# State-space groups: output products of the third and fourth pair, norm and scaling in a later slot, scaling placed behind the products of the inputs

## The reference

```python
proj = h @ in_w                                  # z, xBC, dt
xBC = silu(causal_depthwise_conv(xBC, conv_w, conv_b))   # 4 taps
xs, Bm, Cm = split(xBC)
dt = softplus(dt + dt_bias);  A = -exp(A_log)
# one chunk of 256 tokens per sequence, for each group and head:
cb = einsum("blgn,bsgn->blsg", Cm, Bm)
y = einsum("blsgk,bsgkp->blgkp", cb[..., None] * decay, xs * dt[..., None])
y = (y + xs * D_skip) * silu(z)
yg = y.reshape(bsz, L, 8, -1)                    # 512 features per group
yg = yg * rsqrt(mean(square(yg), -1) + eps);  y = yg * norm_g
return y @ out_w
```

## Time and profile before

| | |
|---|---|
| time, median of 3 runs | 3548.23 us (3548.18 to 3550.38) |
| time of the profiled execution | 3549.42 us |
| its span | 3547.6 us |
| PE / PEld busy | 3447.0 us (97%) / 3381.8 us (95%) |
| DVE / ACT / POOL busy | 2783.1 us (78%) / 1987.5 us (56%) / 587.2 us (17%) |
| mean granted clock of TensorE | 0.995 of full speed |
| part of the span with the state-space groups 1 to 7 and the projections behind them | about 2275 to 2895 us |

### The profile page before, as it was taken

The page is one execution under the profiler, slowest core; times in us unless marked ns, Lnnn a source line. Parts: engine busy times, 40 slices in busy tenths (PEclk is TensorE's granted clock), DMA queues, the critical chain, the costliest instruction groups (busy, mean ns, idle before and its releaser), DMA issues.

```text
span 3547.6 us, 68240 instructions
## 1 busy us (share of the span) xinstructions
PE 3447.0 (97%) x27858; PEld 3381.8 (95%) x27858; DVE 2783.1 (78%) x4529; ACT 1987.5 (56%) x3204; POOL 587.2 (17%) x546
## 2 busy tenths in 40 slices
PE   7999999999999999999999999999999998999997
PEld 7999999999999998999999999999999998999997
DVE  7788888577797887877888887898989867666665
ACT  6555546566547676565555546665656746434344
POOL 2111112111113011131111112231313300000000
PEclk9999999999999999999999999999999999999999
DMA  6555556444465444655555565556464543555552
GB/s 239 217 197 219 217 227 231 176 155 179 165 251 203 172 169 173 267 185 218 201 221 202 208 262 180 178 175 230 171 233 169 186 169 146 210 189 199 204 190 107
DMA packets 113688, 699.61 MB, mean 197 GB/s; under 512 B 13216, under 2 KB 29792, under 8 KB 31456
## 3 DMA queue, kind: packets, MB, share of 16 engines
q1 hardware_dynamic: 104128, 685.14, 52.2%
q10 hardware_dynamic: 8784, 8.46, 1.0%
q0 software_dynamic: 464, 1.64, 0.1%
HBM read 684.64 MB, written 2.16 MB: 194 GB/s over the span
## 4 chain that ended last, share of the span: by engine, by line
PE 49%; DVE 13%; ACT 6%; issue 2%; DMA 1%; POOL 1%; DVEq 0%; SPq 0%; POOLq 0%; ACTq 0%
PE g L446 15%; PE g L448 15%; PE g L447 15%; DVE w_lo L1594 4%; ACT w_hi L1026 2%; DMA w_raw<-in_slots 1%; POOL scratch L2409 1%; DVE vec L2095 1%; DVE rstd L2095 1%; PE turn_bank L485 1%; DVE scratch L1659 1%; DVE scratch L2121 0%; DVE scratch L2129 0%; PE norm_bank L459 0%; DVE h L2225 0%
## 5 line engine op out<-in xcount | busy, mean ns | idle before, releaser
L1594 DVE TENSOR_TENSOR w_lo<-w_raw,w_hi 128x1024 fp32r<-128x1024 f32 x1088 | 1337.0, 1232 | 433.9 <-ACT w_hi L1026 423.1
L1026 ACT ACTIVATE w_hi<-w_raw 128x1024 fp32r<-128x1024 f32 x1088 | 1129.6, 1053 | 873.2 <-PE g L448 761.7
L446 PE MATMUL g<-p_hi,w_hi 128*128 128x256 f32 x4576 | 1318.0, 288 | 36.4 <-DVE w_lo L1594 23.2
L448 PE MATMUL g<-p_hi,w_lo 128*128 128x256 f32 x4576 | 1296.2, 283 | 0.0
L447 PE MATMUL g<-p_lo,w_hi 128*128 128x256 f32 x4576 | 1296.2, 283 | 0.0
L446 PE MATMUL g<-q_hi,w_hi 128*128 128x256 f32 x3408 | 980.0, 288 | 5.7 <-DVE w_lo L1594 2.2
L448 PE MATMUL g<-q_hi,w_lo 128*128 128x256 f32 x3408 | 964.0, 283 | 0.0
L447 PE MATMUL g<-q_lo,w_hi 128*128 128x256 f32 x3408 | 963.8, 283 | 0.0
L446 PEld LDWEIGHTS g<-p_hi,w_hi 128*128 128x128 f32 x4576 | 879.1, 192 | 46.1 <-DVE w_lo L1594 32.7
L447 PEld LDWEIGHTS g<-p_lo,w_hi 128*128 128x128 f32 x4576 | 879.3, 192 | 1.4
L448 PEld LDWEIGHTS g<-p_hi,w_lo 128*128 128x128 f32 x4576 | 879.0, 192 | 0.0
(11 more groups left out here) (445 smaller groups left out, 3929.2 us busy)
## 6 DMA issues: line engine op xcount, KB each, us to landing
w_raw<-in_slots SPq DMA_DIRECT2D x640, 1024.0 KB, 4.9
scratch<-scratch SPq DMA_DIRECT2D x128, 64.0 KB, 4.9
scratch<-s_rows ACTq DMA_DIRECT2D x16, 256.0 KB, 3.4
con<-s_rows ACTq DMA_DIRECT2D x16, 256.0 KB, 5.1
h<-in_x SPq DMA_DIRECT2D x4, 512.0 KB, 6.2
out_h<-h SPq DMA_DIRECT2D x4, 512.0 KB, 2.6
sq<-in_p POOLq DMA_DIRECT2D x4, 256.0 KB, 3.0
con<-in_consts SPq DMA_DIRECT2D x1, 832.0 KB, 10.7
```

The source lines that it names most:

```text
L446: pe.matmul(g, wh, hi[:, k], start=n == 0, stop=False)
L448: last = pe.matmul(g, wl, hi[:, k], start=False, stop=n == len(ks) - 1)
L1026: act.activation(w_hi[k % SPLIT][:, cols], raw[MAIN_AT[k] % RAW][:, cols], ACT.Copy).then_inc(hi_ready, 1)
L1594: dve.tensor_tensor(w_lo[k % SPLIT][:, cols], raw[MAIN_AT[k] % RAW][:, cols], w_hi[k % SPLIT][:, cols], SUB).then_inc(lo_ready, 1)
```

## The change

The steps of the group before are moved, for groups 1 to 7. `S_OUT`, the steps in which the four output products (and the sums, squares and additions behind them) are done, goes from (0, 1, 3, 4) to (0, 1, 4, 5). The norm (PE, and ACT's `factor`) goes from step 5 to 6, `s_scale_y` (DVE) and `s_y_hi` (ACT) from step 6 to 7, `s_y_lo` (DVE) from the start of step 7 to the start of step 8. In step 7 DVE does `s_previous`, that is, the scaling, behind `s_inputs` and no longer ahead of it. For the last group's work, which is done during the last projection, the steps stay as they were (`S_OUT_TAIL`). No instruction is added or removed; each engine has as many rows as before. In the changed program the lines of the functions are 2 to 8 higher.

```diff
--- before.py
+++ after.py
@@ -137,7 +137,7 @@
 
 LN_TILES = [[] if n < 6 else [2 * n - 12, 2 * n - 11] if n < 12 else [n] for n in range(DT)]
 
-S_OUT = (0, 1, 3, 4)
+S_OUT, S_OUT_TAIL = (0, 1, 4, 5), (0, 1, 3, 4)
 
 A_SLOTS = 8 * A_HEADS
 PLE_SLOTS = 1 + DT + 8 + 1 + 8
@@ -815,9 +815,11 @@
 
         def s_previous(g, step, turned):
 
-            if step in S_OUT:
-                s_out(S_OUT.index(step), turned)
-            if step == 5:
+            tail = g == S_GROUPS - 1
+            outs = S_OUT_TAIL if tail else S_OUT
+            if step in outs:
+                s_out(outs.index(step), turned)
+            if step == (5 if tail else 6):
                 s_norm()
 
         def s_norm():
@@ -1390,13 +1392,15 @@
                 last.then_inc(scaled_h, 1)
 
         def s_previous(g, step):
+            tail = g == S_GROUPS - 1
+            outs = S_OUT_TAIL if tail else S_OUT
             if step < 2:
                 s_fetch(g, step + 2)
-            if step in S_OUT:
-                s_square(S_OUT.index(step))
-            if step == 5:
+            if step in outs:
+                s_square(outs.index(step))
+            if step == (5 if tail else 6):
                 factor(rsn[:, 2], "eps_5")
-            if step == 6:
+            if step == (6 if tail else 7):
                 s_y_hi(g)
 
         def s_group(g):
@@ -2136,9 +2140,11 @@
             dve.tensor_tensor(q_lo[:, four], s_y, q_hi[:, four], SUB).then_inc(x_lo, 1)
 
         def s_previous(g, step):
-            if step in S_OUT:
-                s_y_out(g, S_OUT.index(step))
-            if step == 6:
+            tail = g == S_GROUPS - 1
+            outs = S_OUT_TAIL if tail else S_OUT
+            if step in outs:
+                s_y_out(g, outs.index(step))
+            if step == (6 if tail else 7):
                 s_scale_y(g)
 
         def s_steps(n):
@@ -2157,7 +2163,7 @@
 
         def s_group(g):
             for n in range(10):
-                if g and n == 7:
+                if g and n == 8:
                     s_y_lo(g - 1)
                 begin()
                 if g == 0:
@@ -2165,10 +2171,12 @@
                 x = take(columns=n == 1 and g in (3, 5))
                 dve.tensor_copy(s_xbp[:, n % 2, 3:3 + SEQ] if n < 6 else s_z[:, n - 6], x).then_inc(tile_taken, 1)
                 lo_half(1)
-                if g:
+                if g and n != 7:
                     s_previous(g - 1, n)
                 if 4 <= n <= 7:
                     s_inputs(g, n - 4)
+                if g and n == 7:
+                    s_previous(g - 1, n)
                 if n < 6:
                     s_conv(g, n)
                 else:
@@ -2523,11 +2531,11 @@
             else:
                 pool.tensor_tensor(acc[:], acc[:], rsn[:, m % 2], ADD).then_inc(s_sum, 1)
 
-        def s_previous(step):
+        def s_previous(step, outs=S_OUT):
             if step in (2, 3):
                 s_weights(step)
-            if step in S_OUT:
-                s_add_square(S_OUT.index(step))
+            if step in outs:
+                s_add_square(outs.index(step))
 
         def s_group(g):
             for n in range(10):
@@ -2546,7 +2554,7 @@
             for g in range(S_GROUPS):
                 s_group(g)
             for step in range(5):
-                s_previous(step)
+                s_previous(step, S_OUT_TAIL)
 
             c.next("tile", 1 + 10 * S_GROUPS + DT * S_PAIRS)
             c.next("norm")
```

## The result

The changed kernel takes 3556.31 us (median of 11 runs, 3554.02 to 3559.43), the kernel before 3548.18 us beside it (11 runs, 3545.65 to 3550.38). The ratio is 1.0023, 95% interval 1.0015 to 1.0031: slower by 8.1 us. The profiled execution of the changed kernel took 3559.43 us, its slowest.

The account below looks back on a forecast made before the run. Two loops were taken as tight at once: PE's, and DVE and ACT's through the decay-row loads. Seven delays of 1.6 us less 2.9 us of slack gave +8.3 us, 3556.5 us; range 3549 to 3563.

Parts of the forecast that it names:

- Steps 1 and 2: PE's stalls before L812 (3.0 us) and at step 7's transposes (10.9 us) go; PE could gain 13.9 us.
- Step 3: Norm stays one step behind the fourth output product; costed at nothing in a first group.
- the circle: DVE and ACT loop from scaling through `q_hi`, decay-row loads, decay and `w_hi` to the next group: 65.47 us a group.
- Step 4: DVE's scaling comes 5.62 us later, behind the inputs of pairs 2 and 3 and other work.
- Step 5: On ACT the loads queue behind `s_y_hi`, which waits for the scaling: issued 1.84 us later, passed in full to the decay.
- d: Delay per group on DVE's and ACT's loop: 0.9 to 2.3 us, taken as 1.6.
- the slack of 0.93 us: DVE's waits for PE through ACT at step 1, taken off the delays: 0.40, 0.18, 0.35 us in groups 2, 4, 6.
- The sum: Delays over three segments of the layer, less slack: 2.8, 3.0 and 2.5 us, together +8.3 us.
- the 2.0 us of slack in the last projection: DVE's take of the second tile there could be 2.0 us late before PE's tile wanting it waits.
- Full gain, 3534.3: Rival: PE's stalls go and nothing takes their place, gaining all 13.9 us; chance 0.14.
- The lock gives time back, 3553: Rival: fewer DVE collisions with POOL at the new places, 0.9 to 1.2 us a group, +3.4 to +5.5; chance 0.14.
- New waits inside the group: Rival: PE late with step 7's tile delays the scaling by up to another 0.6 us a group, 3562; chance 0.10.

Follow-up runs that it names:

- e5: Changed kernel with decay-row loads issued in step 6 (groups 1 to 7), `s_y_hi` moved to step 8, `s_y_lo` to the start of step 9: 3534.65 us.
- e7: e5 with `q_lo` behind the take and low half of step 9, except in groups 2 and 4: 3537.71 us.
- e1: Changed kernel with ScalarE's two loads of decay rows in step 7 issued ahead of `s_y_hi`, not behind it: 3547.25 us.
- e8: Changed kernel run once more, unaltered: 3558.41 us.
- e4: Kernel before with only DVE's inputs of pair 2 put ahead of the scaling in step 6, nothing a step later: 3555.68 us.
- e6: Changed kernel with the scaling ahead of the inputs again, in its new step 7: 3555.33 us.
- e3: Kernel before with the first two loads of decay rows issued in step 6, ahead of `s_y_hi`, in groups 1 to 7: 3548.56 us.

## Why the prediction was right, point by point

The forecast was 3556.5 us; 3556.31 was measured, and the sum of +8.3 us against +8.1 by the medians and +8.7 by the stretch. That is closer than its terms deserve: two of them were off in opposite directions and nearly cancelled, which is luck.

- **Steps 1 and 2, what PE could gain.** 13.9 us. Right, and shown: e5 keeps the change, takes the loads and the copy out of the way, and its stretch is 13.9 us shorter.
- **Step 3, the norm at nothing in a first group.** Nearly: PE waits 3.9 us in five groups for the squares (L2532). While the circle is the longer loop these waits should cost nothing, since the circle's delay below is the whole loss; no run takes them out alone. In e7, where the circle is open, 2.8 us of such waits are nearly all that is left, and it is 3 us above e5.
- **Step 4, the scaling 5.62 us later.** The order of DVE's work was read rightly; the collisions took some off. From the output product to the end of the scaling it was 36.76 us in group 6 and is 2757.45 + 1.66 - 2717.43 = 41.68: 4.92 later. Of the 0.70 us that are missing, the scalings give 0.50 (2.16 to 1.66) and the inputs of pair 1 0.49, the inputs of pair 2 take 0.48 back, and DVE's wait for `w_hi` in step 2 is 0.17 shorter (0.74 for 0.91). The durations traded places as a lock has it.
- **Step 5, the loads behind the wait: d.** The mechanism is shown by e1. The size was 1.6 us a group, and it is smaller. The first decays of step 8 give it (the first table behind this list). From group 0 to group 7 they are 551.67 us apart before and 560.38 after: +8.71 us. With the slack of 0.93 us that was used up first, this is 9.64 / 7 = 1.38 us a group; in e8 it is 1.32. By the lock rule of the Trainium skill (SBUF — State Buffer, "Who interferes with whom") it was 1.35, nearer than my middle value. The seven steps are uneven: 1.87, 0.58, 1.90, 0.89, 1.45, 0.46 and 1.56 us. Those into groups 2, 4 and 6 have the slack in them; why the rest differ is open. Group 6 to group 7, from output product to output product, takes 66.3 us, not 67.1.
- **The sum.** Seven delays of 1.38 us less 0.93 give 8.7 us, and the stretch is 8.7 us longer: the circle's delay came through whole. The step that failed is the 2.0 us of slack in the last projection. DVE's take of the second tile there (L2186) was to be late by up to 2.0 us at no cost. The second table behind this list holds it against the end of the stretch. Where the clock does not fall at that place (e1, e4, e6), the stretch is longer by 1.5 to 1.6 us less than the take is late; in the changed kernel, where it falls, by 0.1 us less. So there was a slack of 1.6 us and not 2.0, because the z tile of step 9 has to be taken first, which I left out: there PE waits 2.12 us (L2172). And the fall behind that wait, which no step of mine priced, used it up. That it was the fall rests on this comparison of five kernels; the fall can't be switched off by itself. A middle value too large by 7 x 0.22 = 1.5 us and a slack of 2.0 us that gave nothing came out near the same sum.
- **The other two falls.** They cost nothing on top. Without a fall PE waits twice more in the projection behind group 2, for DVE's tiles of `h`. In e4 it is 0.45 and 0.57 us (the rows stand behind the tables). Counted from the wait of group 0 and held against the kernel before, PE comes out of that projection 2.55 us late in e4 and 4.20 in the changed kernel, and DVE's first take in it (L2188, L2194) is 2.56 and 4.21 late: with a fall or without one, PE ends as late as DVE came.
- **The waits by name.** The stalls before L812 for POOL and at step 7's transposes went, the latter in all seven groups. That PE would wait 2 to 4 us a group at the transposes of steps 5 and 6 was wrong: there it is 1.5 us in all. PE meets the late DVE earlier, at the output product of step 1, at the norm and, at the projections, at the z tile. ACT's wait for the rows in group 6 is 0.83 us and not over 1, since the transfer took 0.3 us less there; its decay still comes 44.99 us behind the output product, 0.9 later.

Start of the first decay (ACT, four of 128x128) in step 8 of each group, us, from ACT's timelines:

| group | 0 | 1 | 2 | 3 | 4 | 5 | 6 | 7 |
|---|---|---|---|---|---|---|---|---|
| before | 2270.29 | 2334.89 | 2400.62 | 2513.12 | 2578.69 | 2691.02 | 2756.84 | 2821.96 |
| changed | 2268.72 | 2335.19 | 2401.50 | 2515.90 | 2582.36 | 2696.14 | 2762.42 | 2829.10 |

The last projection, us later than in the kernel before, both from the end of the wait in group 0 (DVE's take before: 2835.96 - 2245.50 = 590.46 us); a fall behind that first wait is left in:

| kernel | fall at the last projection | DVE's take of the second tile | end of the stretch | given back |
|---|---|---|---|---|
| e1 | no | -0.37 | -1.93 | 1.56 |
| e4 | no | 7.65 | 6.10 | 1.55 |
| e6 | no | 9.39 | 7.83 | 1.56 |
| changed | yes | 10.46 | 10.39 | 0.07 |
| changed again (e8) | yes | 8.19 | 8.11 | 0.08 |

The takes of the second tile in e6 and in the changed kernel:

```profile
2841.78 0.47 DVE L2192 SCALAR_TENSOR_TENSOR h<-g,mod,h 128x256 f32<-128x256 f32 x1
```

```profile
2843.07 0.47 DVE L2194 SCALAR_TENSOR_TENSOR h<-g,mod,h 128x256 f32<-128x256 f32 x1
```

PE's two waits for `h` in e4, early in the projection behind group 2:

```profile
2413.94 0.39 PE L446 MATMUL g<-q_hi,w_hi 128*128 128x256 f32 x1 [0.45 <-DVE h L2188]
...
2417.65 0.36 PE L446 MATMUL g<-q_hi,w_hi 128*128 128x256 f32 x1 [0.57 <-DVE h L2188]
```

**The rivals.** *Full gain, 3534.3*: false for this change, because of the order on ACT; e5, which alters that order and keeps the rest, gets there with 3534.65. *The lock gives time back, 3553*: the durations moved as that rival wants, but d of 1.38 lies above its 0.9 to 1.2, and its sum took off the slack as well. *New waits inside the group*: they are there (L459), and the circle stays at 66.3 us, where this rival had 67.7 or more. What the scaling costs by being a step later, and what by standing behind the inputs, is not the sum of two: either alone, e4 (+7.0 us) and e6 (+5.9), costs nearly what both cost together (+8.1).

## What to carry to other kernels

An instruction that waits is a gate for all that is issued behind it on its engine, DMAs too. Before a producer is moved later, look at who waits for it and what stands behind that wait; here three small reorderings on the waiting side turned +8 us into -15. Where two loops are about equally long, freeing one alone shows nothing (e3 frees the circle; no run frees PE's loop without lengthening the circle), and the worth of an edit can only be read when the other is free as well. And a slack must be measured to the first thing that the late engine owes, not to the one that the eye is on; and it can be used up by a slower clock behind the wait itself.

## What the hardware showed unexpectedly

TensorE's granted clock falls after single short waits in a stream that is otherwise dense. Behind the waits of 1.76 to 2.12 us at the projections of the changed kernel it fell six times of six, and behind one of 3.18 us in e6 as well; behind the same wait of 1.9 us in group 0 five times of ten, and five times of ten behind one of 2.1 us just after the stretch; behind e4's three output products of 2.24 us, once. Behind waits of 1.2 to 1.6 us within the stretch it never fell, 14 of them at the transposes of the kernel before and of e3. So the length of the wait alone does not say whether a fall comes; what else does was not tried. At each fall the clock took 1.7 us, nearly as much as the wait before it. In two places of three that time stood where PE would have waited anyway, and in the third it used up 1.6 us of slack.

The second is e6's: loads of 256 KB that were issued 1.1 us earlier landed 1.0 us slower on the mean, so that an earlier issue was worth nothing.
